# The first mixer's other order on ScalarE and VectorE, and half 1's features behind the experts transposed without their root

## What is computed

```python
# first block, token_mixer
c_gate, b_gate, x_in, q, k, v, o, i_pre, f_pre, ga, gm = split(h @ w_in)
ya = b_gate * causal_dwconv(c_gate * x_in, conv_a_w)
qk = silu(causal_dwconv(concatenate([q, k]), conv_qk_w))
hm = mlstm(q, k, v, ig, fg);  hm = hm * rsqrt(mean(hm * hm) + EPS) * mh_norm_w
ym = sigmoid(o) * hm
mix = sigmoid(ga) * (ya @ w_branch_a) + sigmoid(gm) * (ym @ w_branch_m)
# first block, end: x = x + g2 * rms_norm(peer(h), norm2_post)
# second block
h = x * rsqrt(mean(x * x) + EPS) * norm1_g
q, k, v, xl, gl = split(h @ w_in)
q = rms_norm(q per head) * q_norm_g;  k = rms_norm(k per head) * k_norm_g
xl = causal_depthwise_conv(xl, conv_w, conv_b)
lru = rg_lru(xl) * gelu(gl)
x = x + concatenate([attention(q, k, v), lru]) @ w_out
```

## Time and profile before

| what | value |
|---|---|
| median of 3 runs | 1303.18 us (1302.99 to 1303.56) |
| profiled execution | 1302.74 us |
| its span, first to last instruction | 1300.9 us |
| PE busy | 1155.2 us, 89% |
| DVE busy | 912.5 us, 70% |
| ACT busy | 503.5 us, 39% |
| GpSimd busy | 326.6 us, 25% |
| mean granted TensorE clock | 0.966 of 2.4 GHz |

### The profile page before, as it was taken

One profiled execution on the slowest core, in us unless ns is written; L12 is line 12 of the kernel. 1 busy time (PEld: TensorE's weight loads), 2 busy tenths in 40 slices (PEclk: granted clock), 3 DMA queues, 4 the chain that ended last, 5 costly groups with the idle time before them and its releaser, 6 DMA issues.

```text
span 1300.9 us, 15410 instructions
## 1 busy us (share of the span) xinstructions
PE 1155.2 (89%) x5438; PEld 817.6 (63%) x5438; DVE 912.5 (70%) x1874; ACT 503.5 (39%) x974; POOL 326.6 (25%) x310
## 2 busy tenths in 40 slices
PE   5889999999889989987877978787888999999998
PEld 5878898999755545443333433333334897899887
DVE  6875687788787777767677767776756696666544
ACT  4545435445432322122221222221524477555432
POOL 4000000000145654544454455434441000000000
PEclk8899999999999999999999989899998999999999
DMA  9753367677799999999999999999996632445551
GB/s 362 306 215 141 103 223 275 227 299 268 304 421 425 423 427 424 426 427 426 426 426 427 427 426 426 426 427 426 427 425 290 222 110 78 174 171 175 210 193 38
DMA packets 57697, 405.68 MB, mean 312 GB/s; under 512 B 6908, under 2 KB 7108, under 8 KB 9108
## 3 DMA queue, kind: packets, MB, share of 16 engines
q0 software_dynamic: 38576, 272.49, 49.9%
q1 hardware_dynamic: 19044, 132.19, 27.2%
HBM read 403.61 MB, written 1.05 MB: 311 GB/s over the span
## 4 chain that ended last, share of the span: by engine, by line
PE 38%; DMA 32%; DVE 15%; ACT 7%; issue 6%; POOL 1%; SPq 0%; DVEq 0%; ACTq 0%; POOLq 0%
DMA gbuf<-in_peer_uv,ei 17%; DMA ring<-in_peer_uv,ei 11%; PE bank L825 8%; DVE half L1497 5%; PE bank L481 4%; PE bank L477 4%; PE bank L478 4%; ACT half L1042 4%; DMA row_place<-in_peer_uv,ei 3%; PE bank L1016 2%; PE bank L1018 2%; PE bank L1017 2%; PE bank L752 2%; PE bank L492 1%; PE bank L498 1%
## 5 line engine op out<-in xcount | busy, mean ns | idle before, releaser
L1497 DVE TENSOR_TENSOR half<-ring,half 128x1024 fp32r<-128x1024 f32 x175 | 212.7, 1223 | 137.3 <-ACT half L1042 137.1
L825 PE MATMUL bank<-gbuf,dg 128*128 128x512 f32 x540 | 257.3, 621 | 50.8 <-ACT dg L1313 50.7
L1923 DVE CUSTOM_DVE_ANT_0 gbuf<-gbuf,h2t 128x1024 f32<-128x1024 f32 x135 | 165.6, 1227 | 85.4 <-DMA gbuf<-in_peer_uv,ei 84.5
L825 PEld LDWEIGHTS bank<-gbuf,dg 128*128 128x128 f32 x540 | 104.2, 197 | 191.4 <-issue 119.6
L1042 ACT ACTIVATE half<-ring 128x1024 fp32r<-128x1024 f32 x175 | 182.7, 1051 | 89.8 <-PE bank L1018 45.6
L2253 POOL DMA_INDIRECT gbuf<-in_peer_uv,ei x135 | 157.0, 1163 | 189.7 <-PE bank L825 113.8
L825 PE MATMUL bank<-ring,dg 128*128 128x512 f32 x356 | 171.5, 619 | 26.8 <-ACT dg L1313 26.8
L1305 ACT ACTIVATE za<-za 128x4 f32<-128x4 f32 x62 | 12.7, 205 | 402.8 <-DVE za L1923 402.8
L2253 POOL DMA_INDIRECT ring<-in_peer_uv,ei x89 | 108.2, 1216 | 166.3 <-DVE ei L1896 70.6
L1923 DVE CUSTOM_DVE_ANT_0 ring<-ring,h2t 128x1024 f32<-128x1024 f32 x89 | 108.8, 1225 | 53.7 <-DMA ring<-in_peer_uv,ei 53.5
L825 PEld LDWEIGHTS bank<-ring,dg 128*128 128x128 f32 x356 | 69.3, 198 | 118.0 <-issue 80.0
(11 more groups left out here) (432 smaller groups left out, 1947.8 us busy)
## 6 DMA issues: line engine op xcount, KB each, us to landing
ring<-in_weights SPq DMA_DIRECT2D x114, 1024.0 KB, 4.8
gbuf<-in_weights SPq DMA_DIRECT2D x4, 1024.0 KB, 9.8
gbuf<-in_peer_uv,ei POOLq DMA_INDIRECT x135, 23.3
wq_place<-in_weights SPq DMA_DIRECT2D x2, 1024.0 KB, 6.9
bcs<-in_b_ada POOLq DMA_DIRECT2D x3, 512.0 KB, 12.2
ring<-in_peer_uv,ei POOLq DMA_INDIRECT x89, 23.1
xs<-in_x SPq DMA_DIRECT2D x2, 512.0 KB, 8.1
ya<-in_weights SPq DMA_DIRECT2D x1, 1024.0 KB, 17.1
```

Of the source, the lines that this page charges most:

```text
L825: r = e.matmul(acc[a][j][:, :], dg[:, i % 4, :], expert_rows(i)[:, 1024 + 512 * j:1536 + 512 * j], start=h == 0 and k == 0, stop=h == 7 an ...
L1497: e.tensor_tensor(l, v, h.bitcast(f32), ALU.subtract).then_inc(*o.inc(s_lov, split(n)))
L1923: e.tensor_tensor_reduce(row, row, h2t[:, ITS[n][0], :], 1.0, 0.0, ALU.mult, ALU.add, za[:, n % 2, i % 16:i % 16 + 1]).then_inc(*o.inc(s_d ...
```

## The change

In the first mixer the order on ACT and DVE is changed and nothing is added. v stage: `hi` and `lo` of the third v chunk go ahead of the gates' steps, and the last exponential of the gates moves from behind v0 into v1. c loop: on ACT the `hi` runs three chunks ahead and stands behind the copy of c; on DVE the `lo` of that chunk stands between W and S. b loop: each `hi` stands ahead of the rounding of the `ya` before. The mLSTM norm is taken apart: its sum step and root go into the x loop, reciprocal and scaling into the ga loop.

Behind the experts, half 1's gained x is transposed as it is, before its root is known, so that its hfh and hfl are short of a factor for each token. The factor comes back later: q2 and k2 are normed for each head, and there only EPS is scaled; v2 of half 1 is scaled by it in ACT's copy; for xl and gl, where tokens are columns, a matmul spreads the diagonal over all partitions (`rr`), and DVE multiplies. Ahead of the transposes stand 34 matmuls of 256 columns whose result nobody reads. q2 goes through `token_product`.

```diff
                 frees[4 + 2 * a + j] = ((s_y1, 5 + 2 * a + j), (s_nsq, SQ["y2", 2 * a + j]))
...
-        two = [bank(0), bank(1)]
-        cs_ = []
-
-        def q2_half(a, i0, i1):
-            for g in range(2):
...
-
-        block_features(1, (2, 3))
-        for i in range(4):
-            cs_.append(split_done(chunk_at["q2", i]))
-            for a in range(2):
-                q2_half(a, i, i + 1)
+        def h3_ready(k, a):
+            e.wait_ge(s_fhi, FHI["h3", 2 * a + k // 4])
+            e.wait_ge(s_flv, FLV["h3", 2 * a + k // 4])
+
+        h3_ready(7, 0)
+        pb = bank(0)
+        for _ in range(34):
+            e.matmul(pb[:, 0:256], hfh[:, 0, 0:128], hfh[:, 0:2, 0:128], start=True, stop=True)
+        for g in range(2):
+            pb = bank(2 + g)
+            e.wait_ge(s_hu, 6 + g + 1)
+            feature_half(h2t[:, 1, :], pb, g, "h3", 2 + g)
+            frees[2 + g] = ((s_flv, FLV["h3", 2 + g]),)
+        token_product("q2", 0, 1, hfh, hfl, h3_ready)
         frees[0], frees[1] = ((s_qkt, 1),), ((s_qkt, 2),)
+        pb = bank(4)
+        e.wait_ge(s_rd, 4)
+        e.matmul(pb[:, 0:128], tri[:, 1, :], rd[1], start=True, stop=True).then_inc(*o.inc(s_first, FIRST["rr", 0]))
+        frees[4] = ((s_rr, 1),)
         token_product("k2", 2, 3, hfh, hfl)
...
                 e.activation(qkT[:, 0:4, :], cg[:, 0:4, :], AF.Silu).then_inc(*o.inc(s_silu, 1))
+        hi(chunk_at["v0", 2])
         e.wait_ge(s_gpre, 2)
...
-                taken(f"v{j}", i)
+                if j or i:
+                    taken(f"v{j}", i)
+                if j and i == 1:
+                    e.wait_ge(s_gr, 2)
+                    e.activation(G[2], G[2], AF.Exp, scale=-1.0).then_inc(*o.inc(s_gx, 3))
             for a in range(2):
                 e.activation(vx[:, a, 4 * j:4 * j + 4, 0:128], head_heads(banks[4 - 4 * j + a]), AF.Copy).then_inc(
                     *o.inc(s_v, 2 * j + a + 1))
-            if j == 0:
-                e.wait_ge(s_gr, 2)
-                e.activation(G[2], G[2], AF.Exp, scale=-1.0).then_inc(*o.inc(s_gx, 3))
 
         def mlstm_exp(h):
...
         for f in range(8):
-            taken("c", f)
+            n = chunk_at["c", f]
             if f == 0:
+                hi(n + 2)
                 e.wait_ge(s_silu, 2)
+            e.wait_ge(s_chunk, n + 1)
             e.activation(cg[:, f, :], banks[f % 4][:, 0:256], AF.Copy).then_inc(*o.inc(s_c, f + 1))
+            hi(n + 3)
             mlstm_exp(f)
             if f:
                 mlstm_out(f - 1)
-        for g in range(8):
+        mlstm_out(7)
+        for g in range(1, 8):
             taken("x", g)
-            if g == 0:
-                mlstm_out(7)
-        for g in range(8):
-            taken("b", g)
-            e.wait_ge(s_gate, 1)
-            e.wait_ge(s_ya, g + 1)
-            e.activation(yh[:, g, :], ya[:, g, :], AF.Copy).then_inc(*o.inc(s_fhi, FHI["ya", g]))
-        sqrt(rsm, "hm", 0)
+            if g == 4:
+                sqrt(rsm, "hm", 0)
+        e.wait_ge(s_gate, 1)
+        for g in range(9):
+            if g < 8:
+                for m in ahead(chunk_at["b", g]):
+                    hi(m)
+            if g:
+                e.wait_ge(s_ya, g)
+                e.activation(yh[:, g - 1, :], ya[:, g - 1, :], AF.Copy).then_inc(*o.inc(s_fhi, FHI["ya", g - 1]))
         for j in range(4):
             for i in range(2):
                 taken("ga", 2 * j + i)
...
             hi(WQ0 + 19 + m)
         for wi, nm in enumerate(("q2", "k2")):
             if wi:
+                e.wait_ge(s_first, FIRST["rr", 0])
+                e.activation(rr[:, 128:256], banks[4][:, 0:128], AF.Copy, scale=-1.0).then_inc(*o.inc(s_rr, 1))
...
+            if a:
+                e.wait_ge(s_rd, 4)
+            e.activation(v2[:, a, :], banks[6 + a][:, :], AF.Copy, scale=hs[1][2] if a else 1.0).then_inc(*o.inc(s_v2, a + 1))
...
-        def var(r, ssq, count, *mark):
-
-            e.tensor_scalar(r, ssq, 1.0 / count, EPS, ALU.mult, ALU.add).then_inc(*o.inc(s_var, NORM[mark]))
+        def var(r, ssq, count, *mark, eps=None):
+
+            if eps is None:
+                e.tensor_scalar(r, ssq, 1.0 / count, EPS, ALU.mult, ALU.add).then_inc(*o.inc(s_var, NORM[mark]))
+            else:
+                e.tensor_scalar(r, ssq, eps, 1.0 / count, ALU.add, ALU.mult).then_inc(*o.inc(s_var, NORM[mark]))
...
             conv(cg[:, g, :], pad[:, g, :], cqk_w, g, (8, 4), s_conv)
+        lo(chunk_at["v0", 2])
         e.wait_ge(s_gate, 1)
...
-        def mlstm_scores(h):
+        def mlstm_scores(h, between):
...
+            lo(between)
             e.wait_ge(s_mlw, h + 1)
...
         for f in range(8):
-            for m in ahead(chunk_at["c", f]):
-                lo(m)
-            mlstm_scores(f)
+            n = chunk_at["c", f]
+            if f == 0:
+                lo(n + 2)
+            mlstm_scores(f, n + 3)
             if f:
                 mlstm_den(f - 1)
         for g in range(8):
-            taken("x", g)
+            if g:
+                taken("x", g)
+            e.wait_ge(s_chunk, chunk_at["x", g] + 1)
             e.wait_ge(s_c, g + 1)
...
+            if g == 3:
+                e.wait_ge(s_hm, 8)
+                e.tensor_scalar(rsm, ssm, 1.0 / 128, EPS, ALU.mult, ALU.add).then_inc(*o.inc(s_var, NORM["hm", 0]))
...
         lows("ya", 7, yh, yl, ya)
-        e.wait_ge(s_hm, 8)
-        var(rsm, ssm, 128.0, "hm", 0)
...
+        def memory_normed():
+            e.wait_ge(s_nsd, NORM["hm", 0])
+            e.reciprocal(rsm, rsm).then_inc(*o.inc())
+            e.wait_ge(*o.now)
+            for a in range(2):
+                e.tensor_tensor(hm[:, 8 * a:8 * a + 8, :], hm[:, 8 * a:8 * a + 8, :],
+                                rsm[:, 8 * a:8 * a + 8].unsqueeze(2).to_broadcast([128, 8, 128]), ALU.mult).then_inc(
+                    *o.inc(s_den, 9 + a))
...
+            if j == 1:
+                memory_normed()
...
-            diagonal(a)
+            if a:
+
+                e.wait_ge(s_nsd, NORM["h3", a])
+                e.scalar_tensor_tensor(out=hs[a][0], in0=hs[a][2], scalar=64.0 * EPS, in1=hs[a][2], op0=ALU.mult,
+                                       op1=ALU.mult).then_inc(*o.inc())
+                e.wait_ge(*o.now)
+                rstd(hs[a], "h3", a)
+            else:
+                rstd(hs[a], "h3", a)
+                diagonal(a)
             yield
             for g in range(2):
                 features_lo(a, g, banks[2 * a + g], "h3")
+                if a:
+                    yield
+            if a:
+                diagonal(a)
 
         def lru_rate():
...
         for j, _ in enumerate(experts_norm(1)):
-            if j == 3:
+            if j == 4:
                 lo(WQ0 + 16)
...
-                var(sl, sl, 64.0, nm, a)
+                var(sl, sl, 64.0, nm, a, eps=hs[1][0] if a else None)
...
+            e.wait_ge(s_rr, 1)
+            e.tensor_tensor(xlp[:, f, 131:259], xlp[:, f, 131:259], rr[:, 128:256], ALU.mult).then_inc(*o.inc())
+            e.wait_ge(*o.now)
             conv(xl[:, f, :], xlp[:, f, :], cw2, f, (4, 4), s_xlc, bias=cb2[:, f:f + 1])
...
-            e.tensor_copy(gl[:, f, :], banks[f % 2][:, 0:256]).then_inc(*o.inc(s_gl, f + 1))
+            e.tensor_tensor(gl[:, f, :], banks[f % 2][:, 0:256], rr[:, :], ALU.mult).then_inc(*o.inc(s_gl, f + 1))
```

More of the change, by code:

```diff
@@ L152, in build_program @@
     s_bc = [sem(f"s_bc{i}") for i in range(4)]
+    s_rr = sem("s_root_rows")
     s_x, s_p0, s_p1, s_gbias, s_if, s_bd, s_nb, s_n2, s_out = [sem("s_" + n) for n in (
@@ L200, in build_program @@
         table |= {("h4", 2 * a + g): table["h4", 0] + 2 * g + a for g in (1, 0) for a in (1, 0)}
-    FIRST = counted(("wo", 2), ("q", 2), ("y2", 1), ("wp", 1))
+    FIRST = counted(("wo", 2), ("q", 2), ("y2", 1), ("rr", 1), ("wp", 1))
     W1 = counted(("exp", 1), ("ln", 1), ("w", 4), ("exp1", 1), ("ln1", 1), ("w1", 4))
@@ L345, in build_program @@
     mixT = st("mixT", [128, 8, T])
+    rr = st("rr", [128, T])
     stage.close()
@@ L489, in highs @@
                     if by_k:
-                        by_k(k)
+                        by_k(k, a)
                     s_ = slice(128 * a, 128 * a + 128)
@@ L778, in first_scores @@
             frees[b] = ((s_sct, 1 + c),)
-        def keep_busy(pb, xh, n):
-            for _ in range(n):
-                e.matmul(pb[:, 0:256], xh[:, 0, 0:128], xh[:, 0, :], start=True, stop=True)
         shifts((6, 7))
@@ L954, in wp_part, with mx_ready @@
                  first, between)
-        def mx_ready(k):
+        def mx_ready(k, a):
             if k >= 4:
@@ L1401, in scalar_program @@
         for a in range(2):
-            e.activation(v2[:, a, :], banks[6 + a][:, :], AF.Copy).then_inc(*o.inc(s_v2, a + 1))
+            if a:
+                e.wait_ge(s_rd, 4)
+            e.activation(v2[:, a, :], banks[6 + a][:, :], AF.Copy, scale=hs[1][2] if a else 1.0).then_inc(*o.inc(s_v2, a + 1))
         for f in range(4):
```

(9 more changed lines are left out.)

## The result

The changed kernel takes 1286.88 us (median of 4 runs, 1285.66 to 1290.52) against 1303.37 for the kernel before beside it: ratio 0.9874, 95% interval 0.9863 to 0.9886. The forecast was 1286.1, its range 1282.5 to 1291.0. A second comparison gave 1287.96 against 1304.29, ratio 0.988. The profiled execution took 1287.5 us, its span is 1285.7 and its mean granted clock 0.975.

What follows compares the result with a forecast made beforehand. PE bounds the first mixer from 206.9 us, waiting for ACT ahead of that; gathers bound about 355 to 992 us. Gains 15.0 + 1.8 = 16.8 from 1302.74 give 1285.9, stated as 1286.1 us; range 1282.5 to 1291.0.

Steps and rivals of the forecast that it cites:

- A: First mixer: the new order on ACT and DVE in the v stage, c loop and x to wa gains 15.0 us.
- A, v and c: v stage: 3.9 us idle and 1.7 clock gained, new stall 1.0; c loop: 3.3 idle and 1.5 clock gained.
- A, x to wa: Second x product to first wa product: hi moved ahead and norm steps moved remove 4.1 us of PE idle time.
- The 2.6 us: Norm steps moved into the ga loop: two chunks between a lo and its use cover them; otherwise they cost 2.6 us.
- B: Behind the experts: k2 starts 2.9 us earlier, 1.1 us is lost again on DVE, net gain 1.8 us.
- The rule: Behind the experts: transposes don't count for the clock gate as matmuls do, so the clock might drop right behind them.
- rival 1: Behind the experts the clock falls anyway, at the transposes or within the 34 matmuls: 1289.5 to 1293 us, chance 0.12.
- (2): The c loop's ring through ACT and DVE stays the bound, with a similar stall in b: 1288 to 1290, chance 0.10.
- (4): From v to the mixer's end, PE without pauses isn't granted its clock: 25 us lost, 1311 us, chance 0.02.
- (5): Mixer: moved hi steps wait for their buffer (the product three back), so half the gain: 1293.6 us, chance 0.03.
- rival 3: The v1 stall of 1.0 us and the 1.1 on DVE have unseen cover: 1283.5 to 1284.5 us, chance 0.07.
- the 0.44: Whole kernel: the profiled execution of before, 1302.74 us, is 0.44 under the median of 1303.18.

Runs made afterwards that it cites:

- the two runs: Kernel after with the b loop's old order (1289.31 us), and kernel after with the mLSTM norm whole between b and ga as before (1288.35 us).
- the run of B alone: Kernel before with only the change behind the experts, mixer as before: 1303.2 us against 1304.4, ratio 0.999.
- the kernel with A alone: Kernel before with only the mixer's new order, all behind the experts as before: 1288.37 us against 1304.4, ratio 0.9871.
- the second profile of after: The changed kernel, nothing altered, run once more beside three other kernels: 1287.96 us, ratio 0.988.

## Why the prediction was right

**A, v and c.** Forecast 4.9 and 5.1, measured 4.80 and 4.93. First c 23.80 us behind the first v (said 23.6; the absolute times, 94.16 and 189.68 for wa, carry the late start), iterations of 5.20 to the last, the clock at 1.00, one wait of 0.8 on a `lo` (said 1.0). Undoing the v stage alone gives its 4.80 back. Undoing the c loop alone gives 4.9 back, and 1.7 more for a low clock that in before fell inside the loop.

**A, x to wa.** The term that was mis-sized: forecast 5.1, measured 6.06. The idle time of 4.1 was right. The price of a pause beyond its length was not. Timeline of before at one of them:

```profile
186.21 1.18 PE L481 MATMUL bank<-hh,half 128*128 128x256 f32 x8
187.99 0.38 PE L477 MATMUL bank<-hh,half 128*128 128x256 f32 x1 [0.59 <-ACT half L1042]
188.21 0.28 PE L478 MATMUL bank<-hl,half 128*128 128x256 f32 x1
188.32 0.28 PE L477 MATMUL bank<-hh,half 128*128 128x256 f32 x1
```

The eight matmuls ahead end at 186.21 + 1.18 = 187.39, and unstalled the next one starts 0.16 us ahead of such an end, at 187.23. It started 0.76 later, and its second matmul follows after 0.22 instead of 0.12: the pause cost 0.86 and shows 0.59, so 0.27 more. The prediction counted the 0.16 and left out the late second matmul. The timeline has 0.27 at each of the six waits from x to wa, which makes 4.1 + 1.6 = 5.7. The other 0.4 lies in two products of the b loop (191.06 and 194.14 us) that start 0.1 us late and whose second matmul is as late again, without a wait that the profile shows. Not every pause has this price: with the old c loop (undone alone) a wait of 0.84 us lengthens its iteration from 5.20 to 6.11, by 0.91.

The prediction doesn't say which edit brings what. The expectations of the two runs gave each 2.5 us, and both were wrong (1.5 and nothing). The 2.6 us that the prediction would charge for the norm's steps without cover don't show in their old place either, once the b loop is open.

**B.** k2 17.17 us behind the last expert (said 17.2), 1.10 given back up to the weights (said 1.1), 0.09 more behind them. PE now waits 0.6 us for DVE at the weights (line 894, said about 1). No wait of PE over 0.4 from the last expert to k2, and the clock at 1.00. The sum is right (2.9 - 1.2 = 1.7 us, as the run of B alone has it), the reading behind it only in part: the prediction didn't split the 2.9 between the earlier transposes and the fill. By the runs, with the fill there, the transposes earn 1.0 at k2 and lose 1.1 on DVE, and the fill alone is the gain.

**The rule and rival 1.** The granted clock is 1.00 through the 34 matmuls, the 8 transposes and q2, and in the run without the 34 it is 0.99 in the transposes and falls behind them. The Trainium skill (TensorE: Matmul & The Clock Gate, Part 4) says that transposes don't count as busy for the gate the way matmuls do; the drop in that run agrees with it, and with the idle time ahead as well. Idle time is enough: in the kernel with A alone plain matmuls and no transposes follow 5.21 us of it, and the clock falls too (0.53 over the 3.5 us from 987.16). No run shows a drop that needs the transposes. With matmuls ahead of them 8 transposes cost nothing here. The rival's price of 3.4 to 7.4 us was too high in any case: the run that has the drop loses 0.8. Its 3.4 also counts low clock in which PE stood idle: before's low stretch lasts from about 998.7 to 1005.5 us and PE begins at 1001.06, so 4.4 us of work ran at half speed, and 2.2 us were lost.

**The other rivals.** No stall in c or b (2). PE without pauses has its full clock for 235 us (4). In c each moved `hi` starts right behind the copy; in x and b ACT does wait for the product three back (11 waits, 13.3 us in all), but it is far enough ahead that no wait of PE follows (5). Of rival 3 (better than summed) 0.8 us came, in A, from what pauses cost and not from cover.

**The number.** The recorded total has a slip: 1285.9 and the 0.44 that it names make 1286.4, not 1286.1. The median is 0.8 or 0.5 us from these, less than what one execution varies by (1.8 at the start, 0.9 in the MLP, up to 3 in the experts stage), so that it came this close is in part luck. The stages that repeat add up to a gain of 17.5 us in the second profile of after, against 16.8 forecast and 16.5 and 16.3 by the medians. Where that 1 us goes stays open: the profiles vary by that much only ahead of the first v chunk, in the experts stage and in the MLP, and two profiles with the old mixer are too few to tell an effect from chance there.

## What to carry to other kernels

Where ACT and DVE feed PE in turn, put the conversion of the weights ahead of what waits for PE's results, and count a pause of PE at more than its length (0.27 us more ahead of a product here, 0.07 more in the c loop). Two reorderings that free the same queue don't add up: undo each alone before keeping both. And before idle matmuls are put in a pause, see whether a part of the next product is ready; here that brought 2.4 us on top of the 0.8 that the idle ones brought.

## What the runs showed of the hardware

- A pause of PE of 0.59 us costs 0.86: the last matmul ahead isn't overlapped (0.16 to 0.17), and the second one behind the pause starts 0.10 late.
- Behind 4.15 us of idle time the granted clock was still 0.99 for the first 1.1 us of work and then 0.50 for 3.4.
- DVE rounds 128x1024 to fp32r in 0.70 us, where ACT takes 1.04.
- A low clock inside a loop that waits anyway costs nothing. The last S by v matmuls of the old c loop come 49.03 us behind the first c product in before (clock 0.66 from 135 to 140 us), 49.06 with B alone (0.95 from 100 to 135) and 49.14 with the clock at 1.00 up to there. Behind the last wait such a stretch cost 1.7 us.
